# Where two weight splits stand inside an attention pass: one kernel, 1 core of Trainium2

## The reference, cut to what matters

```python
mod_x = (silu_c @ w_ada[l] + b_ada[l])[:, None, :]        # modulation: 6 x 1024 numbers, same for the context
hx = modulate(rms_norm(x, g_norm1[l]), sh1_x, sc1_x)      # and hc for the context
qa, ka, va, qb, kb, vb, qc, kc, vc = jnp.split(hx @ w_in[l], bounds, axis=-1)
oa, ob, oc = ...                                          # three kinds of attention, 16 heads in all
x = x + gt1_x * (jnp.concatenate([oa, ob, oc], axis=-1) @ w_out[l])
x = x + gt2_x * conv_ffn(modulate(rms_norm(x, g_norm2[l]), sh2_x, sc2_x), ...)
```

## Time and profile before

| | |
|---|---|
| time, median of 3 runs | 2258.08 us (2256.72 to 2259.97) |
| profiled execution | 2255.04 us, of which the span is 2253.2 us |
| PE busy | 2110.4 us |
| DVE busy | 1514.5 us |
| ACT busy | 1150.2 us |
| POOL busy | 561.5 us |
| mean granted TensorE clock | 0.972 |

### The profile page before, as it was taken

One profiled execution on the slowest core, in us unless ns is written; L12 is line 12 of the kernel. 1 busy time (PEld: TensorE's weight loads), 2 busy tenths in 40 slices (PEclk: granted clock), 3 DMA queues, 4 the chain that ended last, 5 costly groups with the idle time before them and its releaser, 6 DMA issues.

```text
span 2253.2 us, 43766 instructions
## 1 busy us (share of the span) xinstructions
PE 2110.4 (94%) x18160; PEld 1970.9 (87%) x18160; DVE 1514.5 (67%) x2244; ACT 1150.2 (51%) x1919; POOL 561.5 (25%) x668
## 2 busy tenths in 40 slices
PE   6999989999999999899999989989997989999997
PEld 5986679999999886689988889989996889998997
DVE  3657766777777666668776769755556677865554
ACT  4535545555655643555556555554444655554443
POOL 0012321332333002213321144104330134212331
PEclk9999999999999998999999999999998999999999
DMA  8546544555555454345544335535552434453552
GB/s 345 178 143 230 206 169 147 191 188 171 168 196 184 140 163 159 129 143 192 191 159 155 131 118 183 179 121 197 188 188 105 158 114 150 144 196 133 190 191 85
DMA packets 103205, 378.37 MB, mean 168 GB/s; under 512 B 11456, under 2 KB 11744, under 8 KB 101984
## 3 DMA queue, kind: packets, MB, share of 16 engines
q1 hardware_dynamic: 101520, 367.31, 47.6%
q10 hardware_dynamic: 1488, 8.27, 1.0%
HBM read 374.49 MB, written 1.05 MB: 167 GB/s over the span
## 4 chain that ended last, share of the span: by engine, by line
PE 33%; issue 13%; POOL 5%; DVE 3%; ACT 3%; POOLq 0%; DVEq 0%; ACTq 0%
PE ps L406 10%; PE ps L408 10%; PE ps L407 10%; POOL R L2596 2%; POOL R L2638 1%; DVE WL L1637 1%; PE ps L481 1%; POOL R L2441 1%; PE ps L420 1%; POOL X L2399 1%; PE ps L421 1%; ACT WH L1005 1%; PE ps L428 1%; DVE RST L1673 1%; DVE TMP L1647 0%
## 5 line engine op out<-in xcount | busy, mean ns | idle before, releaser
L406 PE MATMUL ps<-X,WH 128*128 128x256 f32 x4384 | 1242.6, 283 | 15.3 <-DVE WL L1637 7.9
L407 PE MATMUL ps<-X,WH 128*128 128x256 f32 x4384 | 1228.4, 280 | 0.0
L408 PE MATMUL ps<-X,WL 128*128 128x256 f32 x4384 | 1227.4, 280 | 0.0
L1637 DVE TENSOR_TENSOR WL<-RAW,WH 128x1024 fp32r<-128x1024 f32 (+2 forms) x608 | 773.6, 1290 | 452.9 <-ACT WH L1005 451.1
L406 PEld LDWEIGHTS ps<-X,WH 128*128 128x128 f32 x4384 | 827.0, 189 | 30.0 <-DVE WL L1637 11.7
L407 PEld LDWEIGHTS ps<-X,WH 128*128 128x128 f32 x4384 | 826.9, 189 | 1.7
L408 PEld LDWEIGHTS ps<-X,WL 128*128 128x128 f32 x4384 | 826.9, 189 | 0.0
L1005 ACT ACTIVATE WH<-RAW 128x1024 fp32r<-128x1024 f32 (+2 forms) x608 | 623.8, 1045 | 263.6 <-PE ps L408 261.5
L2441 POOL TENSOR_SCALAR R<-CONS,SM 128x128 f32<-128x128 f32 x128 | 83.8, 666 | 319.6 <-DVE SM L1832 308.9
L2535 POOL TENSOR_TENSOR TMP<-TMP 128x256 f32<-128x256 f32 x66 | 48.9, 741 | 446.6 <-ACT TMP L1354 443.1
L1155 ACT ACTIVATE PB<-ps,SM 128x512 f32<-128x512 f32 (+1 forms) x152 | 87.6, 583 | 140.9 <-DVE SM L1822 140.5
(11 more groups left out here) (194 smaller groups left out, 2204.0 us busy)
## 6 DMA issues: line engine op xcount, KB each, us to landing
RAW<-w_dram SPq DMA_DIRECT2D x674, 512.0 KB, 3.7
RAW<-w_dram SPq DMA_DIRECT2D x16, 480.0 KB, 3.2
BIG<-big_dram ACTq DMA_DIRECT2D x4, 1024.0 KB, 5.2
RAW<-w_dram SPq DMA_DIRECT2D x8, 320.0 KB, 2.7
RAW<-w_dram SPq DMA_DIRECT2D x6, 384.0 KB, 2.9
XT<-x_dram ACTq DMA_DIRECT2D x2, 1024.0 KB, 7.5
CONS<-con_dram ACTq DMA_DIRECT2D x1, 1169.0 KB, 9.7
out_dram<-XT SPq DMA_DIRECT2D x1, 1024.0 KB, 3.9
```

The source lines that it names most:

```text
L406: e.matmul(out, a.hi, b.hi, start=start and i == 0, stop=False, skip_group_check=open_bank)
L407: e.matmul(out, a.hi, b.lo, start=False, stop=False, skip_group_check=open_bank)
L408: last = e.matmul(out, a.lo, b.hi, start=False, stop=stop and i == n - 1, skip_group_check=open_bank)
L1637: e.tensor_tensor(weights(i).lo, raw(i), weights(i).hi.bitcast(F32), ALU.subtract).then_inc(*w_lo.mark(i))
```

## The change

`ada_step` inside attention is called with `ahead` 0, on ScalarE and on VectorE, so it no longer reaches tiles beyond itself. In slots that have no step, every second one (odd `calls[0]`) asks for one more tile: ScalarE for the next one at once, VectorE for the one that ScalarE was asked for two slots before.

```diff
# ScalarE
                     def ada_next():
                         if k.ada_n[l, st]:
                             k.ada_n[l, st] -= 1
-                            ada_step(k.ada)
+                            ada_step(k.ada, 0)
+                        elif calls[0] % 2:
+                            feed.reach(max(feed.cut, feed.n) + 1)
# VectorE
                     def ada_next():
                         if k.ada_n[l, st]:
                             k.ada_n[l, st] -= 1
-                            ada_step(k.ada)
-
+                            ada_step(k.ada, 0)
+                        elif calls[0] % 2:
+                            feed.reach(due[0])
+                            due[0] = max(due[0], feed.n) + 1
+
+                    due = [0]
                     ada_turn()
                     attend(tag, heads(l, st), k.one, k.inv, False, out_of, ada_turn, (subnorm, ada_next))
```

## The result

The changed kernel takes 2245.2 us (median of 6 runs, 2242.85 to 2249.94), against 2256.4 us for the kernel before, run beside it (6 runs, 2254.59 to 2259.97). The ratio is 0.9954, with a 95% interval of 0.9941 to 0.9967: faster by 10 us, or 0.5%. The profiled execution took 2244.61 us, its span 2242.8 us, its mean granted clock 0.972.

The account below looks back on a forecast made before the run. TensorE, busy for 94% of the span, was taken to set the time. The terms gave -3.4 us in (0,1) and -4.3 in (1,0), together -7.7, plus 1.4 for one clock fall: -6.3, hence 2251.8 us, range 2248 to 2256.

Parts of the forecast that it names:

- Part 1: Ends of (0,1) and (1,0): row copy comes earlier, cutting the turning's gaps of 3.29 and 2.16 us; -4.4 us.
- Part 2: Half clock behind the turning's gaps in (0,1) and (1,0) goes: 1.0 and 1.4 us, -2.4 us in sum.
- Part 3: Splits in attention slots without a step delay the values (line 643): +1.8 us, bounds 0 and 5.9.
- The full length of the splits: Rival: VectorE's splits in attention slots cost all 5.9 us, not 1.8; total 2255.9 us, chance 0.17.
- VectorE against GpSimd: A split meeting a GpSimd diagonal could cost up to 0.6 us more; nothing was added for it.
- Part 4: Start of out projection: fewer low parts before the first residual, line 481's wait shrinks by 1.17 and 1.4 us; -2.6 us.
- TensorE runs without gaps behind this point: Behind the out projection's first residual: given as reason that little speaks for a gain smaller than 2.6 us.
- Part 5: Tails of (0,1) and (1,0): new waits bring one clock fall, +1.4 us, bounds 0 and 3.4.
- my own sign of being wrong: Prediction wrong if line 643's waits grow over 4 us in all, or one half-clock stretch loses over 1.7 us.
- The clock term as a whole: Both attention tails: two falls of 1.7 us less and one more, -1.7 us of lost work.
- The range: Whole kernel: 2248 to 2256 us, with 1.5 us either side for medians of few runs.
- The no-fall rival: Attention tails stay busy enough, so no new clock fall: -7.7 us, 2250.4 us, chance 0.22.

Follow-up runs that it names:

- Copyfirst: Kernel before, with only VectorE's copy of the modulation row moved ahead of the two low parts, which stay in the last step's slot: 2250.73 us, ratio 0.9973.
- tail: Changed kernel with VectorE's low parts in slots 15, 16 of (0,1) and 12, 15, 16 of (1,0): 2244.21 us, ratio 0.9946; repeated, 2247.11 us.
- cap2: Changed kernel with splits inside attention limited to two tiles, the others staying at the out projection's start: 2248.84 us, ratio 0.9956 to the kernel before.
- again: The changed kernel unaltered, run once more with its own trace: 2245.66 us, ratio 0.9957 to the kernel before.
- only01: The change in pass (0,1) alone, pass (1,0) as in the kernel before: 2255.52 us, ratio 1.0.
- only10: The change in pass (1,0) alone, pass (0,1) as in the kernel before: 2252.06 us, ratio 0.998.
- the delays by hand: Useless products added near 1000 us: changed kernel with 10 more 2248.3 us, with 20 more 2251.7; kernel before with 25 more 2258.6 (means).

## Why the prediction was wrong in size

**Part 1, right.** 1.0 us left in (0,1), none in (1,0). Copyfirst shows the cause by itself. I gave no reason for the 1.0 us that stays. The timelines show a part of it: ahead of the row's copy stand the two low parts of line 2029 (now 2031) with the slow 1.48 us of the earlier trace rows, 1.49 in the changed kernel, where the other pass has 0.86.

**Part 2, right in the place.** The granted clock is 1.00 in both windows, in all six traces of the changed kernel and in copyfirst. The price of 1.0 and 1.4 us was not measured by itself.

**Part 3, right.** Forecast were waits of line 643 of about 2.1 and 1.7 us; 1.88 and 1.53 were measured, and a total of +1.0 and +0.9 us on line 643 where I had +1.08 and +0.68. The full length of the splits, 5.9 us, is refuted. On VectorE against GpSimd: two low parts of line 2031, 1.49 us in copyfirst, were as long as in the earlier trace rows, and in tail a split of 1.44 us at 307.17 stands where the others took 1.22. So a split can be held up by 0.2 us, but none of the changed kernel's splits in these slots was: all took 1.21 or 1.22 us. (The Trainium skill, SBUF — State Buffer, "Who interferes with whom", would have a meeting of the two cost up to the whole of the other instruction; the traces here show 0.2 to 0.6 us. The 0.6 us of line 2029 stand ahead of the copy that TensorE waits for, before and after the change alike, so the change gains or loses nothing by them.)

**Part 4, right in the stage, and wrong in one sentence.** Both waits of line 481 went, and cap2 brings them back. But I wrote "TensorE runs without gaps behind this point", and put everything behind the out projections at nothing. That is the step that failed. Behind the out projections of (1,0) TensorE has a gap of 3.6 us, for the normalisation (line 420 waits for ScalarE's line 1087), and the clock falls there. Directly ahead of that gap it waits for the last squares, which the change makes shorter. TensorE's timeline, of before and then of again (the changed kernel):

```profile
976.78 0.70 PE L481 MATMUL ps<-PB,CONS 128*128 128x256 f32 x2 [1.26 <-ACT PB L1044]
...
969.32 0.70 PE L481 MATMUL ps<-PB,CONS 128*128 128x256 f32 x2 [0.59 <-ACT PB L1044]
```

And the windows around the gap, in the same order:

```profile
970.00:990.00 20.00, 15.16 (x102) 14.33 (x102) 13.71 (x27) 9.08 (x18) 0.00 (x0) 0.83 0.30 106
...
970.00:990.00 20.00, 16.41 (x130) 16.42 (x130) 17.07 (x30) 11.42 (x19) 2.74 (x3) 0.91 0.28 90
```

In the kernel before 0.17 x 20 = 3.4 us are lost there, and so in all four of its traces; in four of the six of the changed kernel it is half, 0.09 x 20 = 1.8 us. In the mean that is 3.4 - (4 x 1.8 + 2 x 3.4) / 6 = 1.1 us of lost work, and the third stage is 1.1 us shorter. Over the traces of all kernels the two go together: with the wait of 1.2 to 1.3 us (the four of before, only01, copyfirst and cap2) 3.4 us are lost in all seven, with the one of 0.59 us in two of eleven. Cap2 differs from the changed kernel only in the two tiles fewer, so the wait is the likely cause of the longer fall; the two exceptions show that it is not the only one.

The other place is the next gap ahead of line 420, 3.4 us long at 1178 us in the kernel before. TensorE's waits around it are the same in before and again (3.4 us for ScalarE there, 1.8 us for line 406 behind it), and the clock is not. The windows of before and of again:

```profile
1168.00:1190.00 22.00, 17.26 (x110) 16.16 (x109) 15.30 (x28) 12.21 (x23) 2.71 (x3) 0.84 0.19 67
...
1168.00:1190.00 22.00, 19.88 (x137) 18.85 (x138) 15.60 (x23) 12.18 (x24) 2.71 (x3) 0.92 0.33 107
```

Where it is 0.84, two more falls follow by 1250 us in six of seven traces. Then 8.5 us are lost between products 6000 and 7000, which take 157 us; in the other traces 1.7 us (in one 3.4), and they take 153 us. Three of the four traces of before have the long form, and one of the six of the changed kernel, which makes the -2.2 us of the last stage in the table. So few could be chance. But of all traces the long form stands in six, each of which lost 3.4 us at the gap behind the out projections, and in none of the nine that lost less there. No run moved the one fall by itself, so that it brings the other is not shown.

**Part 5, the place right, the size not, and the cause not shown.** The fall stands where I had put it, once, at the end of (0,1), and none in (1,0). I tied it to the new wait, and cap2 has that wait without the fall, so a part of the hit may be luck. The fall loses 3.3 us and not 1.7, though two of the four traces of before lose 3.3 us in that window as well. Its price in time, 2.0 us by cap2, is near the 1.4 us of the sum. By my own sign of being wrong, a stretch of half clock that loses more than 1.7 us, the prediction fails here.

**The clock term as a whole** is thus what was mis-sized: lost work of -1.7 us forecast, -7.0 ± 1.1 measured. By the windows, the tail of (0,1) went from 2.55 us in the mean of the four traces to 3.3 us and the tail of (1,0) from 1.7 to 0, together -0.9 us where I had -1.7; the gap behind the out projections of (1,0) gave -1.1 us. So some 5 us of lost work (7.0 - 0.9 - 1.1) were gained in other places. The stretch from product 6000 to 7000 has 3.7 of them in the traces (6.8 us lost in the mean of before, 3.1 after). Another is the 1.7 us lost at 345 to 353 us in the trace that I predicted from the earlier trace rows, which are in none of the three others of before and in none of the changed kernel, 0.4 us in the mean; the wait there is 1.88 us in before and 1.3 to 1.6 us in the changed kernel. The traces themselves show less than all executions do: by their spans and clocks the six lose 57.2 us in the mean and the four 61.4. Behind the third stage they are 1.5 us shorter in the mean, -2.2 in the stretch named and +0.7 in the rest. Whether the later stages gain because their gaps come earlier, which is what the delays by hand and the missing sum of only01 and only10 hint at, or whether a part of the 7.0 us is the luck of 23 executions, is open.

**The base.** The three runs had a median of 2258.08; 93 runs of the kernel before have 2256.7. That is 1.4 us of the 6.6 us between forecast and result, and the changed kernel's first six runs lie another 0.6 below its median over 23, 2245.8. Against the long averages the miss is 10.7 - 6.3 = 4.4 us.

**The range.** I gave the medians of few runs 1.5 us on either side. Single executions of one kernel lie up to 15 us apart (2248.4 to 2263.1 over 93 runs of before), and my range had no term for falls of the clock anywhere but in the two tails. The no-fall rival, -7.7 us, was nearest, and by luck: the fall that it leaves out came.

## What to carry to other kernels

On an engine that takes its instructions in the order of its queue, as VectorE does in every timeline here, put the short instruction that another engine waits for ahead of the long ones that nobody needs yet, and give a two-engine job a lag long enough that its second half finds its input ready: the first alone was worth 5.7 us here, and without the second the whole gain was lost. A gap of 2 us on TensorE can cost more than 2 us: the one of 2.2 us in pass (1,0) had 1.7 us of lost work behind it in each trace of before. So when gaps are removed or moved, look through all the later gaps for what the clock does behind them, and take the falls from several traces of the kernel before, not from one.

## What the runs showed of the hardware

**The same gap need not bring the same fall.** The same gap of 1.9 us ahead of line 481 at 347 us had a fall behind it in the first trace of the kernel before (0.79 over 345 to 353 us) and none in the three others. The same window of a second execution of the kernel before:

```profile
345.00:353.00 8.00, 5.81 (x46) 5.36 (x45) 5.82 (x12) 4.22 (x7) 0.00 (x0) 1.00 0.22 67
```

The other way round, 250 to 270 us is at 0.83 in the changed kernel's first trace and at 1.00 in the five others, and the wait of 1.9 us at line 643 has a fall behind it in all of these six and none in cap2. Losses come in steps of about 1.7 us: 1.7 or 3.4 behind one gap, and 7.0 or 8.4 from 845 to 880 us. (The Trainium skill, TensorE: Matmul & The Clock Gate, "What's actually happening", says that the number of slow matmuls at a kernel's start differs from one run to the next; here it is so in the middle of the kernel as well.) Part of the 3 us by which executions scatter goes with it: over the 87 of the kernel before, time and lost work have a correlation of 0.66, which is 43% of the variance.

**TensorE has two paces at the full clock.** In the dense stretches one product follows the last by 116.7 ns or by 117.8 ns, 0.9% apart, and these two stretches keep their pace from one gap to the next. The window of the kernel before from 640 to 660 us, to be set beside that of after above:

```profile
640.00:660.00 20.00, 20.00 (x172) 20.00 (x171) 14.67 (x19) 9.86 (x15) 5.47 (x6) 1.00 0.60 203
```

It is the same work at a granted clock of 1.00, yet 172 products against 174. The slower pace held from about 610 to 748 us in this trace, in the changed kernel's first from about 1426 to 1465 us, and in other places in others. Over the 1600 products from 2400 to 4000 it costs 1.1 us (202.2 and 201.1 us in the first traces of before and after), and it shows in no view of the clock; what sets it is not known.
